# The merge stage of a hybrid decoder layer: up-projections from split operands too, and all its weights through one ring of pieces

## What is computed

```python
y_diff = (rmsnorm(y_diff, diff_subln) * (1.0 - lambda_init)).reshape(b, s, DIFF_HEADS * DIFF_V)
g = jax.nn.sigmoid(gates.astype(jnp.float32)).astype(x.dtype)
g_mla, g_diff = g[..., :D_MODEL], g[..., D_MODEL:]
merged = g_mla * (y_mla @ w_up_mla) + g_diff * (y_diff @ w_up_diff)
x = x + merged @ w_out
```

## Time and profile before

| | us |
|---|---|
| median of 3 runs | 2801.51 (2799.98 to 2802.9) |
| the profiled execution's own time | 2797.61 |
| span of the profiled execution | 2795.9 |
| TensorE busy in the span | 2629.9 (94%) |
| merge stage in it, first transpose to the next stage's first product | 637.19 to 936.79 |
| mean granted TensorE clock | 0.973 of full speed |

### The profile page before, as it was taken

The page is one execution under the profiler, slowest core; times in us unless marked ns, Lnnn a source line. Parts: engine busy times, 40 slices in busy tenths (PEclk is TensorE's granted clock), DMA queues, the critical chain, the costliest instruction groups (busy, mean ns, idle before and its releaser), DMA issues.

```text
span 2795.9 us, 43800 instructions
## 1 busy us (share of the span) xinstructions
PE 2629.9 (94%) x14884; PEld 2130.4 (76%) x14885; DVE 1545.9 (55%) x2737; ACT 1114.7 (40%) x1780; POOL 312.9 (11%) x327
## 2 busy tenths in 40 slices
PE   6899989978999998899999999999999999999995
PEld 3356655655666555788888899999999999999994
DVE  5555546764111136777777788885544554454444
ACT  2143424443110022555555666664333333333333
POOL 1000000000000123211111111110111112112111
PEclk9999989999999998999999999999999999999997
DMA  4000010002111441976667777779999999999994
GB/s 143 0 10 5 16 32 16 1 1 69 45 45 45 163 126 50 312 242 211 214 217 217 225 223 242 244 217 287 344 345 341 341 340 341 346 334 341 344 343 167
DMA packets 424685, 527.29 MB, mean 189 GB/s; under 512 B 27845, under 2 KB 334537, under 8 KB 424585
## 3 DMA queue, kind: packets, MB, share of 16 engines
q1 hardware_dynamic: 403544, 464.31, 51.1%
q0 software_dynamic: 20032, 62.11, 9.3%
q10 hardware_dynamic: 1040, 0.00, 0.0%
HBM read 482.23 MB, written 44.14 MB: 188 GB/s over the span
## 4 chain that ended last, share of the span: by engine, by line
PE 57%; DMA 1%; DVE 1%; issue 1%; ACT 0%; POOLq 0%; SPq 0%; POOL 0%; DVEq 0%; ACTq 0%
PE banks L2000 20%; PE banks L2061 17%; PE banks L2010 12%; PE banks L2011 7%; PE banks L1992 1%; DMA acc_rows<-arena,rows 1%; DMA arena<-acc_rows 0%; DVE arena L2370 0%; DMA arena<-h_rows,rows 0%; DVE arena L2374 0%; ACT arena L2215 0%; DVE parts L2265 0%; DVE parts L2248 0%; SPq L1927 0%; DVE arena L2404 0%
## 5 line engine op out<-in xcount | busy, mean ns | idle before, releaser
L2000 PEld LDWEIGHTS banks<-arena 128*128 128x128 f32 x5376 | 603.5, 192 | 1.7
L2000 PE MATMUL banks<-arena 128*128 128x128 f32 x5376 | 603.7, 275 | 0.0
L2010 PE MATMUL banks<-parts 128*128 128x512 f32 (+1 forms) x1536 | 508.5, 374 | 25.0 <-DVE arena L2374 16.7
L2061 PE MATMUL banks<-parts 128*128 128x512 f32 x2064 | 479.4, 391 | 0.0
L2061 PEld LDWEIGHTS banks<-parts 128*128 128x128 f32 x2064 | 384.1, 188 | 78.5
L2011 PE MATMUL banks<-parts 128*128 128x256 f32 x1536 | 436.2, 284 | 0.0
L2261 DVE TENSOR_TENSOR parts<-arena,parts 128x1024 fp32r<-128x1024 f32 x264 | 314.5, 1222 | 59.3 <-ACT parts L2135 59.1
L2010 PEld LDWEIGHTS banks<-parts 128*128 128x128 f32 x1536 | 295.4, 192 | 63.0 <-issue 27.3
L2011 PEld LDWEIGHTS banks<-parts 128*128 128x128 f32 x1536 | 296.2, 193 | 0.2
L2265 DVE TENSOR_TENSOR parts<-arena,parts 128x1024 fp32r<-128x1024 f32 x192 | 234.2, 1223 | 92.9 <-ACT parts L2142 74.8
L2294 DVE TENSOR_SCALAR arena<-banks,arena 128x128 f32<-128x128 f32 x336 | 102.0, 345 | 317.6 <-PE banks L2000 314.0
(11 more groups left out here) (318 smaller groups left out, 3004.0 us busy)
## 6 DMA issues: line engine op xcount, KB each, us to landing
arena<-in_w SPq DMA_DIRECT2D x264, 1024.0 KB, 7.6
arena<-in_w SPq DMA_DIRECT2D x66, 2048.0 KB
arena<-in_w_in SPq DMA_DIRECT2D x27, 512.0 KB, 5.3
arena<-in_x SPq DMA_DIRECT2D x16, 512.0 KB, 8.2
h_rows<-arena POOLq DMA_DIRECT2D x10, 512.0 KB, 7.7
acc_rows<-arena SPq DMA_DIRECT2D x8, 512.0 KB
arena<-acc_rows SPq DMA_DIRECT2D x8, 512.0 KB, 7.3
out<-arena SPq DMA_DIRECT2D x8, 512.0 KB, 6.3
```

The lines of the kernel that those rows point to most:

```text
L2000: last = nc.tensor.matmul(bank(g, 2 * (c % 2) + s)[:, a * JOB:a * JOB + P], w1[c][:, s, k, a * P:(a + 1) * P], xt[:, k, 0:P], start=(k == ...
L2010: nc.tensor.matmul(sums[:, :, 0:rows], first_part[p][:, 0, k, :], x_both[:, :, k, 0:rows], start=(k == 0), stop=(k == KT - 1))
L2061: last = nc.tensor.matmul(bank(g, 2 * c + h), x[:, f, h * P:(h + 1) * P], second_part(q, wide)[:, y, a, :], start=(f == 0 and x is act_hi ...
```

## The change

- The up-projections use split operands as well: y is split into `y_hi` and `y_lo` when it comes out of the banks, the up weights like the gate weights. So each of their blocks takes three fp32r products in place of one plain fp32 product.
- All weights come in pieces of 128 partitions x 4 blocks of k x 128 columns (256 KB), six for each f: up MLA, up diff, gate MLA in two, gate diff in two; 48 in all. Raw pieces go into a ring of four slots, their high and low parts into a ring of three. TensorE does 24 products a piece: 2 halves x 4 blocks x 3. A raw slot is loaded again when the low part of the piece in it is made; a part slot is filled again when TensorE has used its piece.
- Every y bank is read by ScalarE (high) and then by VectorE (low); four banks are used for the transposes, and a group waits for VectorE's subtraction four groups before it. Piece 0, an up piece, is done between the MLA and the diff branch's transposes.
- The loops are written out flat. A gate's half 0 is taken up by ScalarE when it is done, half 1 when its piece is done; VectorE's multiplications follow for each branch, the addition with the second.
- The first three tiles of w_out are loaded after piece 6 into a tile of their own that lies where `stage_out` expects them.
- The arena's segment 2 is given back before the merge stage.

The diff, without the views of memory and the removed lines of TensorE, ScalarE and VectorE (they stand in the code above), with indents halved:

```diff
 def stage_merge(g, io, scope):
...
+w_raw_in = [Since(g.w_head[0], 64), Since(g.w_head[1], 32), Since(g.w_head[2], 32), Since(g.sem("w_merge"), 0)]
+used, made, gated, scaled, merged = (g.sem("merge_" + n) for n in ("used", "made", "gated", "scaled", "merged"))
...
+PIECES = KT * F_PIECES
+half_of = lambda h: slice(h * HALF, (h + 1) * HALF)
+turn_bank = lambda r: bank(g, (0, 1, 4, 5)[r % 4])
...
+def source(p):
+  f, j = divmod(p, F_PIECES)
+  if j < 2:
+    return (w_um, w_ud)[j][:, 0:4, f * P:(f + 1) * P]
+  col = OFF_GATE + (j // 2 - 1) * D + f * P
+  return w_in[:, 4 * (j % 2):4 * (j % 2) + 4, col:col + P]
...
   def _(sp):
-    def load(f, s):
-      for dst, src, col in zip(w[s], (w_in, w_in, w_um, w_ud), (OFF_GATE, OFF_GATE + D, 0, 0)):
-        sp.dma_start(dst, src[:, :, bass.ds(f * P + col, P)]).then_inc(w_tile[s], 16)
-    load(0, 0)
-    load(1, 1)
-    with sp.Fori(1, KT // 2) as i:
-      for s in range(2):
-        sp.wait_ge(made, 4 * i + 2 * s)
-        load(2 * i + s, s)
-    sp.wait_ge(made, 2 * KT)
-    sp.dma_start(at(g, W_OUT, OUT_FIRST * D).rearrange("p (k n) -> p k n", n=D), out_weights(io)[:, 0:OUT_FIRST, :]).then_inc(g.w_out_in[0], 16)
+    for p in range(PIECES):
+      if p >= RAW_SLOTS:
+        sp.wait_ge(w_lo_ready, p - RAW_SLOTS + 1)
+      sp.dma_start(raw[:, p % RAW_SLOTS], source(p)).then_inc(w_raw_in[p % RAW_SLOTS].sem, 16)
+      if p == F_PIECES:
+        sp.dma_start(g.out_first[:, :].rearrange("p (k n) -> p k n", n=D), out_weights(io)[:, 0:OUT_FIRST, :]).then_inc(g.w_out_in[0], 16)
   @block.tensor
   def _(pe):
+    def turn_y(r):
+      b, h, a = r // 8, r // 4 % 2, r % 4
+      if r in (8, 12):
         pe.wait_ge(sub_steps, (NORMED, ALL_NORMED)[h])
+      if r >= 4:
+        pe.wait_ge(copied_d, r - 3)
       for t in range(4):
+        last = nc.tensor.transpose(turn_bank(r)[:, t * P:(t + 1) * P], (y_m, y_d)[b][:, 4 * h + t, a * P:(a + 1) * P], g.ident[:, :])
       last.then_inc(turned, 1)
+    def piece(p):
+      f, j = divmod(p, F_PIECES)
+      pe.wait_ge(w_lo_ready, p + 1)
+      for h in range(2):
+        if j < 2:
+          sums, hi, lo, k0 = bank(g, 4 * h + 2 + j), y_hi, y_lo, 4 * j
+          if f == 0:
+            pe.wait_ge(copied_d, 8 * j + 4 * h + 4)
+          else:
+            pe.wait_ge(scaled, 4 * (f - 1) + 2 * j + h + 1)
+          first, final = True, True
+        else:
+          sums, hi, lo, k0 = bank(g, 4 * h + j // 2 - 1), h_hi, h_lo, 4 * (j % 2)
+          first, final = j % 2 == 0, j % 2 == 1
+        for k in range(4):
+          if j >= 2 and f == 0 and h == 0:
+            pe.wait_ge(h_lo_ready, k0 + k + 1)
+          x_high, x_low = hi[:, k0 + k, half_of(h)], lo[:, k0 + k, half_of(h)]
+          nc.tensor.matmul(sums, part[p % 3][:, 0, k, :], x_high, start=first and k == 0, stop=False)
+          nc.tensor.matmul(sums, part[p % 3][:, 0, k, :], x_low, start=False, stop=False)
+          last = nc.tensor.matmul(sums, part[p % 3][:, 1, k, :], x_high, start=False, stop=final and k == 3)
+        if h == 0 and j in (3, 5):
           last.then_inc(made, 1)
+      last.then_inc(used, 1)
+    for r in range(8):
+      turn_y(r)
+    piece(0)
+    for r in range(8, 16):
+      turn_y(r)
+    for p in range(1, PIECES):
+      piece(p)
   @block.scalar
   def _(act):
+    def high(p):
+      w = w_raw_in[p % RAW_SLOTS]
+      act.wait_ge(w.sem, w.count + 16 * (p // RAW_SLOTS + 1))
+      if p >= 3:
+        act.wait_ge(used, p - 2)
+      nc.scalar.activation(part[p % 3][:, 0], raw[:, p % RAW_SLOTS], ACT.Copy).then_inc(w_hi_ready, 1)
+    def copy_y(r):
+      b, h, a = r // 8, r // 4 % 2, r % 4
+      act.wait_ge(turned, r + 1)
+      dst = y_hi[:, 4 * b + a, half_of(h)]
+      if b == 0:
+        nc.scalar.activation(dst, turn_bank(r), ACT.Copy).then_inc(copied_a, 1)
+      else:
+        nc.scalar.activation(dst, turn_bank(r), ACT.Copy, scale=g.gain_sub[:, 1:2]).then_inc(copied_a, 1)
+    def gate_of(f, b, h):
+      p = F_PIECES * f + 3 + 2 * b
+      if h == 0:
+        act.wait_ge(made, 2 * f + b + 1)
+      else:
+        act.wait_ge(used, p + 1)
+      if f >= 1:
+        act.wait_ge(merged, 2 * (f - 1) + h + 1)
+      nc.scalar.activation(gate[:, 2 * h + b, :], bank(g, 4 * h + b), ACT.Sigmoid).then_inc(gated, 1)
     act.wait_ge(sub_steps, GAIN)
     nc.scalar.activation(g.ssq[:, :], g.ssq[:, :], ACT.Sqrt, scale=1.0 / DIFF_V, bias=g.eps[:, 0:1]).then_inc(sub_steps, 1)
+    for r in range(4):
+      copy_y(r)
+    high(0)
+    for r in range(4, 8):
+      copy_y(r)
+    high(1)
+    for r in range(8, 16):
+      copy_y(r)
     for k in range(KT):
       nc.scalar.activation(h_hi[:, k, :], ht[:, k, :], ACT.Copy).then_inc(h_hi_ready, 1)
+      if k == 3:
+        high(2)
+    for p in range(PIECES):
+      f, j = divmod(p, F_PIECES)
+      if j in (3, 5):
+        gate_of(f, j // 2 - 1, 0)
+        gate_of(f, j // 2 - 1, 1)
+      if p + 3 < PIECES:
+        high(p + 3)
   @block.vector
   def _(dve):
+    def low(p):
+      dve.wait_ge(w_hi_ready, p + 1)
+      nc.vector.tensor_tensor(part[p % 3][:, 1], raw[:, p % RAW_SLOTS], part[p % 3][:, 0], ALU.subtract).then_inc(w_lo_ready, 1)
+    def copy_y(r):
+      b, h, a = r // 8, r // 4 % 2, r % 4
+      dve.wait_ge(copied_a, r + 1)
+      hi, lo = y_hi[:, 4 * b + a, half_of(h)], y_lo[:, 4 * b + a, half_of(h)]
+      if b == 0:
+        nc.vector.tensor_tensor(lo, turn_bank(r), hi, ALU.subtract).then_inc(copied_d, 1)
+      else:
+        nc.vector.scalar_tensor_tensor(out=lo, in0=turn_bank(r), scalar=g.gain_sub[:, 1:2], in1=hi, op0=ALU.mult, op1=ALU.subtract).then_inc(copied_d, 1)
+    def scale(f, b, h):
+      tile = gate[:, 2 * h + b, :]
+      dve.wait_ge(gated, 4 * f + 2 * b + h + 1)
+      nc.vector.tensor_tensor(tile, bank(g, 4 * h + 2 + b), tile, ALU.mult).then_inc(scaled, 1)
+      if b == 1:
+        dve.wait_ge(scaled, 4 * f + 2 + h + 1)
+        nc.vector.tensor_tensor(out[:, f, half_of(h)], gate[:, 2 * h, :], gate[:, 2 * h + 1, :], ALU.add).then_inc(merged, 1)
     nc.vector.tensor_scalar(g.gain_sub[:, 1:2], g.gain_sub[:, 0:1], 1.0 - LAMBDA_INIT, None, ALU.mult).then_inc(sub_steps, 1)
+    for r in range(4):
+      copy_y(r)
+    low(0)
+    for r in range(4, 8):
+      copy_y(r)
     dve.wait_ge(sub_steps, ROOTED)
     nc.vector.reciprocal(g.ssq[:, :], g.ssq[:, :]).then_inc(sub_steps, 1)
     dve.wait_ge(sub_steps, INVERTED)
     for rows in (slice(0, 16), slice(16, 32)):
       nc.vector.tensor_tensor(yv[:, rows], yv[:, rows], g.ssq[:, rows].unsqueeze(2).broadcast_to([P, 16, DIFF_V]),
                   ALU.mult).then_inc(sub_steps, 1)
+    low(1)
+    for r in range(8, 16):
+      copy_y(r)
     for k in range(KT):
       dve.wait_ge(h_hi_ready, k + 1)
       nc.vector.tensor_tensor(h_lo[:, k, :], ht[:, k, :], h_hi[:, k, :], ALU.subtract).then_inc(h_lo_ready, 1)
+      if k == 3:
+        low(2)
+    for p in range(PIECES):
+      f, j = divmod(p, F_PIECES)
+      if j in (3, 5):
+        scale(f, j // 2 - 1, 0)
+        scale(f, j // 2 - 1, 1)
+      if p + 3 < PIECES:
+        low(p + 3)
+    dve.wait_ge(merged, 2 * KT)
...
+w_of = [g.out_first[:, k * D:(k + 1) * D] for k in range(OUT_FIRST)] + [w_out[:, k, :] for k in range(OUT_FIRST, KT)]
...
-          last = nc.tensor.matmul(bank(g, 2 * (t % 2) + h), merged[:, k, t * P:(t + 1) * P], w_out[:, k, h * HALF:(h + 1) * HALF],
+          last = nc.tensor.matmul(bank(g, 2 * (t % 2) + h), merged[:, k, t * P:(t + 1) * P], w_of[k][:, h * HALF:(h + 1) * HALF],
```

More of the change, by code:

```diff
@@ L1272, in stage_merge @@
+    part = [tensor("part0", 2 * HALF, F32R)]
+    y_lo = by_tile(tensor("y_low", KT * SEQ, F32R))
+    h_lo = by_tile(tensor("h_low", KT * SEQ, F32R))
+    h_hi = by_tile(tensor("h_high", KT * SEQ, F32R))
+    part += [tensor("part1", 2 * HALF, F32R), tensor("part2", 2 * HALF, F32R)]
+    part = [a[:, :].rearrange("p (y k n) -> p y k n", y=2, k=4) for a in part]
+    ht = tiled(g, HT, KT, SEQ)
     y_m, y_d = tiled(g, Y_MLA, TT, HALF), tiled(g, Y_DIFF, TT, HALF)
-    h_hi, h_lo = (part[:, :].rearrange("p (k t) -> p k t", k=KT) for part in g.parts[0:2])
@@ L1308, in _ @@
                 for t in range(4):
-                    last = nc.tensor.transpose(bank(g, n % 8)[:, t * P:(t + 1) * P], src[:, 4 * h + t, (a % 4) * P:(a % 4 + 1) * P], g.ident[:, :])
+                    last = nc.tensor.transpose(turn_bank(r)[:, t * P:(t + 1) * P], (y_m, y_d)[b][:, 4 * h + t, a * P:(a + 1) * P], g.ident[:, :])
                 last.then_inc(turned, 1)
[L1311 to L1322, removed]
-                    pe.wait_ge(h_lo_ready, KT)
-                    pe.wait_ge(w_hi_ready, 2 * i + s + 1)
-                    pe.wait_ge(w_lo_ready, 2 * i + s + 1)
-                    for h, cols in enumerate(halves):
-                        for b in range(2):
-                            for k in range(KT):
-                                for c, part in ((0, h_hi), (0, h_lo), (1, h_hi)):
```

(15 more changed lines are left out.)

70 lines of the change are left out of this document (11 added, 59 removed).

## The result

The change makes the kernel slower: 2859.08 us (median of 6 runs, 2856.01 to 2862.97) against 2799.38 us of the kernel before in 6 runs, the three of the table above among them; the ratio is 1.0214, with a 95% interval of 1.02 to 1.0227. The prediction was 2780.0, in a range from 2774 to 2787. The profiled execution took 2857.5 us. One run of the kernel before, among the 13 beside the first experiments, took 4526.27 us at a mean granted clock of 0.55, where the others have 0.97; the ratios leave it out.

A forecast was written before the change was run, and what follows sets the result against it. TensorE alone was taken to set the merge loop's pace. Savings of 20.0 us (loop), 1.2 - 0.3 (beginning) and 0.65 (end) made 21.5 us, taking 2801.5 to 2780.0 us, range 2774 to 2787.

The forecast's parts named there:

- The loop written out: Merge stage: TensorE's code grows from 512 to 2,304 instructions; the trace shows no branch cost to take away, so no gain.
- the slow end of 2820: Merge loop: three part slots refill too slowly and starve TensorE, 2820 us; chance 0.03, shared with split at another rate.
- The last of the signs: Behind the merge stage: a part not as long as now, from an expert row sent elsewhere by changed rounding, would show error.
- The sum: Whole kernel: 20.0 + (1.2 - 0.3) + 0.65 = 21.5 us less, giving 2780.0 us.
- Terms 1 and 2: Merge loop: split up-projections save 2.81 us per f at 0.2272 us a product; from piece 2 on, 20.0 us less.
- Term 3: Merge stage's beginning: VectorE is the bound; piece 2 starts at 661.45 against 662.62, 1.2 us earlier.
- The landing: Merge stage's beginning: first 256 KB weight piece lands late, costing 0 to 1.1 us, taken as 0.3; 5.2 us upper bound.
- Term 4: Merge stage's end: one multiplication fewer after the last product, 0.65 us less of the 3.22 us gap.
- The wait for w_out: Start of the next stage: TensorE's 3.09 us wait for the last 2.5 MB stays, shifted; loading first tiles earlier gains nothing.
- The table: ScalarE's sigmoids in the merge stage: one to sixteen table loads of 1.28 us each, costing nothing either way.
- the clock: Rival, merge stage's beginning: TensorE's clock falls to half for 3.7 us, costing 1.9 us, 2782 us; chance 0.12.
- VectorE's subtraction out of a bank: Rival, merge stage's beginning: each waits for ScalarE, 0.9 us instead of 0.65 to 0.68, costing 3.7 us, 2784; chance 0.12.

The follow-up runs named there:

- the first experiments: Idle instructions in VectorE's merge-stage list: kernel before with 56, 2873.39 us, with 24, 2798.49 us; changed kernel with 24, 2776.52 us, with 128, 2858.2 us.
- after with 24: The changed kernel with 24 idle instructions (increments of an unread semaphore) added to VectorE's list in the merge stage, 3 at each of eight pieces: 2776.52 us.
- with 32: The kernel before with 32 idle instructions added to VectorE's list in the merge stage: 2799.29 us.
- with 40: The kernel before with 40 idle instructions added to VectorE's list in the merge stage: 2868.64 us.
- with 66: The kernel before with 66 idle instructions added to VectorE's list in the merge stage: 2902.61 us.

## Why the prediction was wrong

**The step that failed is "The loop written out".** It asked of the code only whether the branches of the loop that goes were costing anything, looked at TensorE's list alone, and priced the longer code at nothing; measured, the place that the longer VectorE list gives to the expert loop costs 82.6 us (2859.08 to 2776.52). It never asked what the longer lists do to the code behind them. The rule of the skill that stood beside it was weighed on TensorE's merge loop alone, and there it had nothing to say: it speaks of a branch to code that is not held, and the DMA view of the kernel before shows no packet of instructions between 720 and 930 us, so that loop was held. What it bore on was VectorE's expert loop, with its twelve wide and twenty-one narrow jobs. No row of before warns of it: q14 brought no packet in that stage, which says that the loop was held, and not how near it lay to the edge. None of the rivals named it either: the slow end of 2820 was a starved ring, which did not happen. The last of the signs that the prediction named for being wrong, that the part behind the merge stage is not as long as now, did come, but not for the reason given there, an expert row sent elsewhere: the number of products there is unchanged, and 24 idle instructions undo it.

**What the loss is made of.** Taking the branch back of VectorE as the mark of a job: ten wide jobs took 657.2 us before, 671.9 after, 658.7 in after with 24; the 22 that follow, all but the first narrow, 903.7, 971.2 and 903.4. So 13 and 68 us, together 81 of the 82.6 by which the two versions of the changed kernel differ. A narrow job takes 40.4 us when the code is held, which is TensorE's own work without a gap, and 43.8 when it is not. VectorE stands for 16 us at one place of each (223.8 us in 14 waits, above), but most of this is hidden: in TensorE's list of one job two gaps are left, with this form, in the kernel after:

```profile
2208.52 14.52 PE L2047 MATMUL banks<-arena,arena 128*128 128x128 f32 x128
2223.87 7.41 PE L2047 MATMUL banks<-arena,arena 128*128 128x128 f32 x64 [0.82 <-DVE arena L2361]
2233.09 7.41 PE L2047 MATMUL banks<-arena,arena 128*128 128x128 f32 x64 [1.81 <-DVE arena L2361]
2240.34 1.04 PE L2039 MATMUL banks<-ident,arena 128*128 128x128 f32 x8
```

The brackets make 2.6 of the 3.4 us; they count from a modelled end. By their starts the 256 products of L2047 take 2240.34 - 2208.52 = 31.82 us in this job, and before 2225.23 - 2196.64 = 28.59 (where the line is L2000), so 3.2 us stand there:

```profile
2196.64 28.75 PE L2000 MATMUL banks<-arena 128*128 128x128 f32 x256
2225.23 1.04 PE L1992 MATMUL banks<-ident,arena 128*128 128x128 f32 x8
```

**The other steps**, by the changed kernel with 24, in which nothing behind the merge stage is disturbed. Its TensorE timeline:

```profile
635.66 5.54 PE L1324 MATMUL banks<-ident,arena 128*128 128x128 f32 x32 [3.95 <-PEq L995]
...
659.34 0.50 PE L1345 MATMUL banks<-merge_h_high,merge_part 128*128 128x512 f32 x1 [1.65 <-DVE merge_part L1414]
...
912.50 6.77 PE L1614 MATMUL banks<-merge_out_first,arena 128*128 128x512 f32 x12 [2.62 <-PEq L1304]
922.87 11.85 PE L1614 MATMUL banks<-arena,arena 128*128 128x512 f32 x20 [3.60 <-DMA arena<-in_w_out]
```

- The sum: from the first transpose to the next stage's first product 912.50 - 635.66 = 276.84 us, before 299.60; 22.8 less, forecast 21.5. The whole kernel: 24.0 less by the medians (2800.51 to 2776.52), 22.0 by the spans. Its 2776.52 us lie inside the range forecast for the change.
- Terms 1 and 2: from piece 2 on there is no bracket of idle time, and the last product starts at 909.48. 909.48 - 659.34 = 250.14 us for the 1,103 products before it: 0.2268 us each, forecast 0.2272.
- Term 3: piece 2 starts 23.68 us after the first transpose, forecast 24.26 (661.45 less 637.19). The landing that was bounded by 5.2 us took 2.8 to 2.9 for 256 KB; its 0.3 us were not spent.
- Term 4: the gap before the next stage is 2.62 us in place of 3.22, 0.60 less, forecast 0.65. The wait for w_out stays: 10.37 us from the stage's first product to the landing, before 10.18.
- The table: one load on the sigmoid's line in the whole stage, of the one to sixteen left open.
- The rivals: the clock stays at 1.00 from 640 to 912 us, so it did not fall in the beginning (the row of 641 to 642 that the prediction names lies ahead of both holes of before; the two rows of before at the end of this list, behind the holes, show 1.00 as well); VectorE's subtraction out of a bank took its 0.64 us in a row; the ring never starved TensorE.

```profile
640.00:655.00 15.00, 13.93 (x77) 11.13 (x78) 14.97 (x19) 9.82 (x17) 0.00 (x0) 1.00 0.21 51
655.00:662.00 7.00, 5.35 (x24) 4.08 (x24) 7.00 (x8) 7.00 (x9) 0.00 (x0) 1.00 0.23 62
...
700.00:880.00 180.00, 180.00 (x795) 149.08 (x795) 46.64 (x69) 33.86 (x57) 0.00 (x0) 1.00 0.19 49
```

The kernel before, behind its first and behind its second hole:

```profile
645.00:646.00 1.00, 1.00 (x12) 1.00 (x11) 1.00 (x3) 0.47 (x1) 0.00 (x0) 1.00 1.22 290
650.00:652.00 2.00, 2.00 (x6) 0.90 (x5) 2.00 (x3) 2.00 (x3) 0.00 (x0) 1.00 0.03 8
```

So the change is worth some 24 us, and the place that it gave to another loop's code costs 82.6, which leaves the kernel 60 us slower. With 24 idle instructions it is, at 2776.52 us, faster than the kernel before by the 24.

## What to carry to other kernels

A change that makes an engine's list longer in one stage moves that engine's code of every stage behind it. Where a loop of a few hundred instructions stands there, look at the instruction queues in the window of that loop, before and after: here packets in that window went with a loop fetched anew each time round, and with waits called "issue" on that engine. Idle instructions ahead of the loop tell whether a slowdown far from the edit is of this kind. Try more than one count: the slow range here is 27 to 37 instructions long in every 128, so that one step of 24 can land in it again. Whether a shorter loop body cures it was not run.

## What was not expected of the hardware

- VectorE's code comes in packets of 8,192 bytes on q14, and the time repeats with 128 instructions: 2859.08 us for 0, 2776.52 for 24, 2858.2 for 128 added to the changed kernel. Those of q8, which I take for TensorE's by their number, are of about 16 KB (0.75 MB in 46).
- A loop of 293 instructions in the built program (some 335 on the chip by my estimate) runs without a packet for 1,500 us in the one place (the last packet of the kernel before ahead of the closing part comes at 1199.33 us), and with five packets for each job in the other. The three plain stalls for code in a job of after take 3.9 to 6.0 us, though a packet itself moves in 0.3 to 1.0 us.
- Between held and not held there is nothing in steps of eight instructions (2799.29 with 32, 2868.64 with 40), but the slow times with 40 to 66 differ among themselves by 34 us, most of it in the wide jobs (665.7 us for ten with 40, 693.4 with 66); the cause was not traced.
